# Turning the second attention head of a pair by VectorE and DMA as well, in a hybrid decoder layer with a mixture of experts

## What is computed

```python
xn   = rms_norm(x, norm_mix_w)
proj = xn @ w_in                     # six blocks of 512: c_b, c_c, c_h, q, k, v
yc   = c_b * causal_conv3(c_c * c_h)
# eight heads of 64; q and k normed; queries in blocks of 128 that see L keys
z         = qb @ kb.T * scale
log_keep  = where(s < t, log_sigmoid(-z), 0)
suffix    = reverse_cumsum(log_keep shifted by one)
A         = where(s < t, exp(log_sigmoid(z) + suffix), 0)
ya        = A @ vb
x = x + concat(norm(yc), norm(ya)) @ w_out
x = x + hierarchical_moe(rms_norm(x))    # top 1 of 4 groups, top 2 of 8 experts
```

## Time and profile before

| | before |
|---|---|
| median of the runs (3) | 1168.35 us (1167.06 to 1168.88) |
| the profiled execution | 1168.85 us |
| its span | 1166.8 us |
| TensorE busy in the span | 1097.8 us (94%), 5766 products |
| VectorE busy | 900.9 us (77%) |
| ScalarE busy | 718.8 us (62%) |
| mean granted clock of TensorE | 0.976 of full speed |
| attention with the interleaved projection | about 113 to 420 us |
| its first three quarters | about 113 to 337 us |
| the experts | about 560 to 1120 us |

### The profile page before, as it was taken

The page is one execution under the profiler, slowest core; times in us unless marked ns, Lnnn a source line. Parts: engine busy times, 40 slices in busy tenths (PEclk is TensorE's granted clock), DMA queues, the critical chain, the costliest instruction groups (busy, mean ns, idle before and its releaser), DMA issues. The chain is left out here.

```text
span 1166.8 us, 16853 instructions
## 1 busy us (share of the span) xinstructions
PE 1097.8 (94%) x5766; PEld 897.0 (77%) x5766; DVE 900.9 (77%) x1033; ACT 718.8 (62%) x882; POOL 138.3 (12%) x192
## 2 busy tenths in 40 slices
PE   8999999999999899996899999999999999999950
PEld 7887777778777668885788888888888888888840
DVE  4505957678575762567899999999999999999947
ACT  5423545646643571112788888888888888888830
POOL 1001100010000120001010111111111101101000
PEclk9999999999999999998999999999999999999985
DMA  6201231313213353003999999999999999999519
GB/s 218 59 28 45 89 90 54 111 39 106 67 46 95 107 219 131 37 37 115 425 427 419 384 391 393 388 391 387 380 390 389 387 387 375 385 387 380 228 72 378
DMA packets 77115, 275.27 MB, mean 236 GB/s; under 512 B 20752, under 2 KB 51600, under 8 KB 63888
## 3 DMA queue, kind: packets, MB, share of 16 engines
q1 hardware_dynamic: 66272, 253.69, 57.3%
q0 software_dynamic: 9216, 16.80, 3.8%
q10 hardware_dynamic: 1584, 4.20, 0.9%
HBM read 259.57 MB, written 31.85 MB: 250 GB/s over the span
## 5 line engine op out<-in xcount | busy, mean ns | idle before, releaser
L1193 DVE TENSOR_TENSOR e_lo<-W,e_hi 128x1024 fp32r<-128x1024 f32 x384 | 452.4, 1220 | 22.9 <-ACT e_hi L1187 19.8
L1187 ACT ACTIVATE e_hi<-W 128x1024 fp32r<-128x1024 f32 x384 | 403.5, 1060 | 93.8 <-PE ps L1158 91.7
L1156 PE MATMUL ps<-e_hi,xT_hi 128*128 128x512 f32 x512 | 203.1, 397 | 4.5 <-DVE e_lo L1193 3.5
L1158 PE MATMUL ps<-e_lo,xT_hi 128*128 128x512 f32 x512 | 200.4, 391 | 0.0
L1157 PE MATMUL ps<-e_hi,xT_lo 128*128 128x512 f32 x512 | 199.8, 390 | 0.0
L472 PE MATMUL ps<-xnT_hi,w_hi 128*128 128x512 f32 x320 | 129.0, 403 | 1.6 <-DVE u L861 0.6
L472 PE MATMUL ps<-xnT_hi,w_lo 128*128 128x512 f32 x320 | 128.0, 400 | 0.0
L472 PE MATMUL ps<-xnT_lo,w_hi 128*128 128x512 f32 x320 | 125.3, 392 | 0.0
L1156 PEld LDWEIGHTS ps<-e_hi,xT_hi 128*128 128x128 f32 x512 | 96.9, 189 | 23.9 <-DVE e_lo L1193 3.7
L1158 PEld LDWEIGHTS ps<-e_lo,xT_hi 128*128 128x128 f32 x512 | 96.4, 188 | 20.6
L1157 PEld LDWEIGHTS ps<-e_hi,xT_lo 128*128 128x128 f32 x512 | 96.6, 189 | 19.1
(11 more groups left out here) (236 smaller groups left out, 1681.4 us busy)
## 6 DMA issues: line engine op xcount, KB each, us to landing
W<-in_w_dram SPq DMA_DIRECT2D x96, 2048.0 KB, 13.4
w_raw<-in_w_in_dram SPq DMA_DIRECT2D x20, 512.0 KB, 4.1
yy<-y_rows SPq DMA_DIRECT2D x7, 1024.0 KB, 11.9
xt<-in_x_dram SPq DMA_DIRECT2D x8, 512.0 KB, 3.9
w_out_raw<-in_w_out_dram SPq DMA_DIRECT2D x8, 512.0 KB, 7.3
xn_rows<-xn SPq DMA_DIRECT2D x8, 512.0 KB, 2.8
out_dram<-x ACTq DMA_DIRECT2D x7, 512.0 KB, 8.2
x<-in_x_dram SPq DMA_DIRECT2D x2, 1536.0 KB, 10.9
```

The source lines that it names most:

```text
L1156: pe.matmul(o, xs_hi[:, k], e_hi[:, p, cols], start=(k == 0), stop=False)
L1158: mm = pe.matmul(o, xs_hi[:, k], e_lo[:, p, cols], start=False, stop=(k == last))
L1187: act.activation(e_hi[:, p], flat[:, p * D:(p + 1) * D], ACT.Copy).then_inc(s["hi_made"], 1)
L1193: dve.tensor_tensor(e_lo[:, p], flat[:, p * D:(p + 1) * D], e_hi[:, p], ALU.subtract).then_inc(s["lo_made"], 1)
```

## The change

Head 1 of units 1 to 7 of the first three quarters goes the way of head 0: `by_dma(n, h)` now says yes for both heads there (21 units, 84 tiles), and as before for head 0 alone in units 25 to 27. The semaphores `quads_made`, `spread_out` and `exchanged` are doubled, one for each head, and `quad_rows` has four parts instead of two. VectorE turns head 1 into row CB - 1 of `y_mix`, which the convolution fills only in the last quarter. The core of the diff, the rest of which passes h along:

```diff
-        by_dma = lambda n: n < LIGHT and n % NT > 0
+        by_dma = lambda n, h: n % NT > 0 and n < (LIGHT, UNITS - NT)[h]
...
-            return y_mix[:, CB + n // NT, 0:length(n)].rearrange("p (b k i) -> p b k i", b=QUADS, i=QUAD)
+        def quads_turned(n, h):
+
+            return y_mix[:, CB - 1 if h else CB + n // NT, 0:length(n)].rearrange("p (b k i) -> p b k i", b=QUADS, i=QUAD)
...
             for n in range(1, LIGHT):
-                if by_dma(n):
-                    spread(n)
+                for h in range(2):
+                    if by_dma(n, h):
+                        spread(n, h)
                 for part in range(2):
                     for g in groups_in(n - 1, part):
                         if g % 2 and g // 2 + 2 < len(CHUNKS):
                             load_chunk(g // 2 + 2)
-                if by_dma(n):
-                    collect(n)
+                for h in range(2):
+                    if by_dma(n, h):
+                        collect(n, h)
...
                 pe.wait_ge(turned_read, th(n + 1, 0))
-                if by_dma(n):
-                    pe.wait_ge(exchanged, 16 * QUADS * dma_units(n + 1))
+                for h in range(2):
+                    if by_dma(n, h):
+                        pe.wait_ge(exchanged[h], 16 * QUADS * dma_units(n + 1, h))
...
                 project(ticks_by(n, 0), ticks_by(n, 1))
-                turn(n, 1)
+                if not by_dma(n, 1):
+                    turn(n, 1)
...
-                if n and h == 0 and by_dma(n - 1):
-                    act.wait_ge(quads_made, dma_units(n))
+                if n and by_dma(n - 1, h):
+                    act.wait_ge(quads_made[h], dma_units(n, h))
                 elif n:
                     act.wait_ge(turned, th(n - 1, h) + halves(n - 1))
...
-                if h or not by_dma(n):
+                if not by_dma(n, h):
                     return
-                if dma_units(n):
-                    dve.wait_ge(spread_out, 16 * dma_units(n))
-                dve.wait_ge(weighed, 2 * n + 1)
-                dve.transpose(quads_turned(n).rearrange("p b k i -> p k b i"), s.rearrange("p (k b i) -> p k b i", b=QUADS, i=QUAD)).then_inc(quads_made, 1)
+                if dma_units(n, h):
+                    dve.wait_ge(spread_out[h], 16 * dma_units(n, h))
+                dve.wait_ge(weighed, 2 * n + h + 1)
+                dve.transpose(quads_turned(n, h).rearrange("p b k i -> p k b i"),
+                              s.rearrange("p (k b i) -> p k b i", b=QUADS, i=QUAD)).then_inc(quads_made[h], 1)
```

More of the change, by code:

```diff
@@ L77, in hymba_moe_layer @@
     y_rows = nc.dram_tensor("y_rows", (PAIRS, D), F32, kind="Internal").ap()
-    quad_rows = nc.dram_tensor("quad_rows", (2, P * S), F32, kind="Internal").ap()
+    quad_rows = nc.dram_tensor("quad_rows", (4, P * S), F32, kind="Internal").ap()
     with ExitStack() as ctx:
@@ L228, in hymba_moe_layer @@
         turned_read = sem("turned_read")
-        quads_made = sem("quads_made")
-        spread_out = sem("spread_out")
-        exchanged = sem("exchanged")
+        quads_made = [sem(f"quads_made{h}") for h in range(2)]
+        spread_out = [sem(f"spread_out{h}") for h in range(2)]
+        exchanged = [sem(f"exchanged{h}") for h in range(2)]
         valued = sem("valued")
@@ L292, in hymba_moe_layer, with quads, quads_home @@
         assert all(z_first[n] % 2 == 0 for n in range(UNITS) if halves(n) == 2)
-        by_dma = lambda n: n < LIGHT and n % NT > 0
-        dma_units = lambda n: sum(by_dma(m) for m in range(n))
-        th = lambda n, h: sum((2 - by_dma(m)) * halves(m) for m in range(n)) + h * (1 - by_dma(n)) * halves(n)
+        by_dma = lambda n, h: n % NT > 0 and n < (LIGHT, UNITS - NT)[h]
+        dma_units = lambda n, h: sum(by_dma(m, h) for m in range(n))
+        th = lambda n, h: sum((not by_dma(m, i)) * halves(m) for m in range(n) for i in range(2)) + h * (not by_dma(n, 0)) * halves(n)
         QUAD = 32
         QUADS = P // QUAD
-        def quads_turned(n):
-            return y_mix[:, CB + n // NT, 0:length(n)].rearrange("p (b k i) -> p b k i", b=QUADS, i=QUAD)
-        def quads(n):
+        def quads_turned(n, h):
+            return y_mix[:, CB - 1 if h else CB + n // NT, 0:length(n)].rearrange("p (b k i) -> p b k i", b=QUADS, i=QUAD)
+        def quads(n, h):
             L = length(n)
-            return quad_rows[dma_units(n) % 2, 0:P * L].rearrange("(p c) -> p c", c=L)
-        def quads_home(n):
-            return probsT[0].rearrange("p k t -> p (k t)")[:, 0:length(n)].rearrange("p (a k i) -> p a k i", a=QUADS, i=QUAD)
+            return quad_rows[2 * h + dma_units(n, h) % 2, 0:P * L].rearrange("(p c) -> p c", c=L)
+        def quads_home(n, h):
+            return probsT[h].rearrange("p k t -> p (k t)")[:, 0:length(n)].rearrange("p (a k i) -> p a k i", a=QUADS, i=QUAD)
         TB = lambda g: ps[:, 4 + g % 2]
@@ L358, in mix_sp, with spread, collect @@
                     sp.dma_start(router_b[:, NG:], b_expert.partition_broadcast(P)[:, 0, :]).then_inc(router_in, 16)
[L359 to L364, removed]
+            def spread(n, h):
+                sp.wait_ge(quads_made[h], dma_units(n + 1, h))
+                sp.dma_start(quads(n, h), quads_turned(n, h).rearrange("p b k i -> p (b k i)")).then_inc(spread_out[h], 16)
+            def collect(n, h):
+                sp.wait_ge(spread_out[h], 16 * dma_units(n + 1, h))
                 sp.wait_ge(valued, n)
                 for b in range(QUADS):
-                    sp.dma_start(quads_home(n)[b * QUAD:(b + 1) * QUAD].rearrange("j a k i -> j a (k i)"),
-                                 quads(n).rearrange("(a j) (b r) -> b j a r", a=QUADS, b=QUADS)[b]).then_inc(exchanged, 16)
+                    sp.dma_start(quads_home(n, h)[b * QUAD:(b + 1) * QUAD].rearrange("j a k i -> j a (k i)"),
+                                 quads(n, h).rearrange("(a j) (b r) -> b j a r", a=QUADS, b=QUADS)[b]).then_inc(exchanged[h], 16)
             for c in range(2, PRE + 2):
@@ L536, in values @@
                         head = slice((2 * p + h) * HD, (2 * p + h + 1) * HD)
-                        mm = pe.matmul(ps[h * HD:(h + 1) * HD, VB, (t % 4) * P:(t % 4 + 1) * P], v[:, j, head], quads_home(n)[:, :, j] if by_dma(n) and h == 0 else probsT[h][:, j, :],
+                        mm = pe.matmul(ps[h * HD:(h + 1) * HD, VB, (t % 4) * P:(t % 4 + 1) * P], v[:, j, head], quads_home(n, h)[:, :, j] if by_dma(n, h) else probsT[h][:, j, :],
                                        start=(j == 0), stop=(j == t))
@@ L567, in mix_pe @@
                     values(n - 1)
-                if not by_dma(n):
+                if not by_dma(n, 0):
                     turn(n, 0)
                 project(ticks_by(n, 0), ticks_by(n, 1))
-                turn(n, 1)
+                if not by_dma(n, 1):
+                    turn(n, 1)
                 if r == JOIN[p]:
```

## The result

| | before | with the change |
|---|---|---|
| median (4 runs each) | 1167.97 us | 1177.94 us (1175.09 to 1179.74) |
| ratio to before, 95% interval | | 1.0074 [1.0057, 1.0091] |
| the profiled execution, its span | 1168.85, 1166.8 us | 1179.74, 1177.3 us |
| mean granted clock | 0.976 | 0.964 |

Slower by 0.74%, some 8.7 us (the two medians of four runs are 10.0 us apart, 0.85%, which lies within the interval too); on the 1168.35 of before that is 1177.0, the very end of the stated range, where 1172.7 was forecast. The profiled execution is 10.9 us longer than the one of before, so it shows the losses on the large side: its mean granted clock is 0.964, and 0.966 to 0.970 in the three others, which are 0.9 to 4.7 us shorter.

What follows compares the result with a forecast made beforehand. TensorE's own work was taken to bound the three quarters. -10.0 + 2.5 + 2.1 + (2.0 + 2.1) x 2 + 0.8 + 0.8 = +4.4 us on 1168.85; with the median 0.5 lower, 1172.7, range 1167.0 to 1177.0.

Steps and rivals of the forecast that it cites:

- What bounds the kernel, what is removed and what is added: Three quarters: TensorE sets the time; 10.0 us of its turns go; VectorE gets 15.0 us, SP 21 stores and 84 fetches.
- Unit 1, +2.5: Value products of unit 1: TensorE stalls 4.9 us for head 1's fetches in place of the earlier 2.4, +2.5 us.
- Units 9 and 17, +2.0 each: Value products of units 9 and 17: TensorE waits for head 1's fetches, +2.0 us at each.
- rival D: Unit 1: clock falls behind the 4.9 us wait, 1.6 us lost but absorbed by the bank wait; unabsorbed 1174.3; no chance given.
- The clock, +0: The sum's allowance for a clock fall behind unit 1's wait: a fall expected, but no price.
- Units 3, 11 and 19, +2.1 each: Projection there: late chunk load delays VectorE's low part of q, so TensorE stalls for the bank, +2.1 us each.
- Unit 14, +0.8: Unit 14: the existing 0.6 us wait grows by VectorE's turns of 3 and 2 tiles in front, +0.8 us.
- The load, +0.3: The chunk's load, issued close behind head 1's store, takes 0.3 us more than the earlier 4.06 from issue to cast.
- Loops 15 and 23, given +0.4 each: Units 15 and 23: the bank is late by the late chunk load, about +0.4 us each.
- sum of +5.0: Whole change: by the skill's rule, VectorE's 15.0 us counted in full against TensorE's 10.0, +5.0 us.
- A: Rival, the cover holds: load and bank never late, only units 1, 9 and 17 stall; -3.5 us, 1164.9; chance 0.15.
- C: Rival, the queue takes over: load waits behind stores, units 4, 5, 12, 13 also stall; +10.9 us, 1179.2; chance 0.15.

Runs made afterwards that it cites:

- e2: The change with head 1 of units 1, 9 and 17 turned by TensorE again, the chunk's load still late; ratio 1.0039 to the kernel before.
- e1: The change with SP issuing the chunk's load before the store of head 1 instead of behind it; ratio 1.0050 to the kernel before.
- e3: The change with both edits: load ahead of head 1's store, and head 1 of units 1, 9 and 17 turned by TensorE; ratio 0.9959 to before.
- e4: The kernel before plus VectorE's 21 turns of head 1, their result unused and no further DMA; ratio 1.0024 to the kernel before.
- e11: The same kernel as e3, measured again; ratio 0.9973 to the kernel before.
- e5: e1 with TensorE's waits for fetches in units 1, 9 and 17 filled with turns of a constant tile; ratio 1.0045 to the kernel before.
- e12: e2 with VectorE making the chunk's low part after head 1, the load still late; ratio 0.9998 to the kernel before.
- e8: The change with VectorE making the chunk's low part after head 1 instead of between the heads; ratio 1.0038 to the kernel before.
- e9: e3 with VectorE making the chunk's low part after head 1; ratio 0.9963 to the kernel before.
- e7: e3 with the value products moved behind the first 8 products of the projection; ratio 1.0141 to the kernel before.
- e10: e3 with head 1 by DMA only in units 3 to 7 of each quarter, units 1 and 2 turned by TensorE; ratio 0.9972 to the kernel before.

## Why the prediction was right in direction and short in size

**What bounds the kernel, what is removed and what is added**: as forecast. TensorE was the bound, the turns cost 0.10 us each (loops without a stall are shorter by about that: loop 4 by 0.6, loop 9 by 0.8), and the question was the margin of the fetches and of the bank.

**Unit 1, +2.5**: the sum had loops 1 and 2 together 1.0 us longer (2.5 less the 1.5 of the turns of units 1 and 2); they are 3.9 longer. The start of the value products was met within 0.9 us. Two things were missing. The scores of unit 3 waited 1.9 us for ScalarE's `soft`, since ScalarE may open head 1 of unit 2 only after VectorE's turn of unit 1; this fell into the time that the value products would have waited anyway, and the two waits make 5.9 us instead of 4.9. And the half clock, 1.9 us.

**Units 9 and 17, +2.0 each**: with the clock, the step that failed most. The stalls were 3.0 each. Head 1's store was issued at 202.65 in place of 202.0, the last of the eight fetches went out at 206.8 instead of 205.8, and they landed 2.7 to 3.2 us after their issue instead of 2.4. And the clock fell behind these as well, which rival D had considered for unit 1 alone. Loops 9 and 10 lost 4.4 us together, 17 and 18 3.3, against 0.5 (2.0 less 1.5 for the turns of two units) each in the sum.

**The clock, +0**: rival D said that the clock would fall behind unit 1's wait and cost nothing further, because TensorE would then wait for the bank anyway. In loops 2 and 3 that did hold: the fall cost 1.9 us, and the bank stall of 2.1 us in loop 3 went. But the sum had no clock at units 9, 17 and 14, where it fell too. In all the fall cost 8 us of the profiled execution.

**Units 3, 11 and 19, +2.1 each**: didn't occur in the change. VectorE was on time (q's low part starts at 147.85 and ends at 148.5, the walk had 148.0), but TensorE began loop 3 at 146.1 and not at 143.4, by 1.0 us more of waiting and 1.9 of half clock, and found the bank ready. e2 shows that these stalls are real once units 1, 9 and 17 are mended (5.5 us in all, 6.3 forecast). The losses of neighbouring loops cover one another in part, so e1 and e2 take back 2.8 and 4.1 us alone and 12 to 13 together.

**Unit 14, +0.8**: the wait was 1.5 instead of 0.6, as forecast, but the clock fell behind it too, and the loop lost 2.2. The same wait of 1.5 us in e3 left the clock at 1.00, and the loop at 8.5. Nor is the wait the load's doing: with the load first it is the same.

**The load, +0.3**: undersized. From issue to cast it took 4.1 to 6.1 us in the nine places where it followed a store of head 1, 5.0 in the mean, not 4.4. With the load first (e1) the mean is still 4.8, so that store isn't the whole reason. Loops 15 and 23, given +0.4 each, had waits of 0.3 and 0.8 us that loops 15 and 23 of e1 don't have.

**The total.** Loops 1 to 23 grew by 8.8 us where the sum had 4.4. Of the difference 3 us are the waits of units 1, 9 and 17, each 1 us longer than forecast, and 1.6 us the clock in loop 14. That it isn't larger, and that the result still lies at the very end of the range, is in part luck: 6.3 us of bank stalls in the sum hardly came, and 6.4 us of half clock in loops 2, 10 and 18 stood in for them, of which only loop 2's had been thought of.

**The rules.** VectorE's 15 us cost 2.8 us when added alone (e4), not 15, and with both edits the kernel in which VectorE and the DMAs turn head 1 of 18 units is 3 to 5 us faster than the one in which TensorE does (e3, e11). The forecast had worked out a sum of +5.0 beside the rule in the Trainium skill's "VectorE: DVE Perf Modes", section "Rules for kernel authors", that a 128x128 transposition belongs on TensorE. It is nearer to the change than the forecast's own +4.4, but by chance. Per tile TensorE is the quicker engine here too (0.099 us against 0.16); it was also the one with no time left.

The granted clock fell to 0.50 behind three waits of 3 to 4 us, and e5 shows a price for it. That agrees with the warning of the Trainium skill, "TensorE: Matmul & The Clock Gate", section "Why this matters for your kernels", against pauses between bursts of products. The fall behind 1.5 us in loop 14 comes after a shorter pause than that section warns of.

**The rivals.** A (the cover holds, -3.5) has the number that e3 measures, -3.2 to -4.8, but by another sum: e3 doesn't send units 1, 9 and 17 by DMA at all, where A had 6.5 us of stalls there. C (+10.9) is nearer in total, for another reason: the queue was a partner in it (unit 9's fetches at about 3 us), not the bound in every second unit, and loops 4, 5, 12 and 13 didn't stall.

## What to carry to other kernels

Before work is moved from the engine that is the bound onto a chain of others, write for each moved step when it is ready and when it is due, on every in-order queue it passes, and look at what stands behind it there: here two edits, one of SP's order and one of which units take the new way, turned +8.7 us into -3 to -5. Stalls of neighbouring steps don't add up but cover one another, so an experiment that mends one can show little; try the pair before a cause is dropped. And before a difference between two profiled executions is put down to an edit, compare the waits and the granted clock loop by loop: a fall of the clock may be in one and not in the other. Last, an independent transfer with slack should be issued ahead of stores that wait for compute, not between them and the fetches that are due.

## What the runs showed that I had not expected

The length of a wait alone doesn't say whether the clock falls. Behind 1.5 us in loop 14 the granted clock of TensorE fell to half in the change and in e12 and stayed full in e1, e2, e3, e5, e8, e9 and e11, with the same wait in the same place. Behind the 2.4 to 2.6 us in loop 1 it stayed full in the kernel before, in e3, e4, e7, e9, e11 and e12 and fell in e2 and e10. What decides it was not found. Filled with turns of a constant tile, waits of 3 to 4 us left it at 1.00 (e5). And the fetches of 96 KB landed 1.2 us later when a load of 512 KB was issued just before them. The DMA share is under one half over the three quarters (0.40 in e12), which hides this: while those fetches were under way it was 1.07.
